# fp32r products for gather and spread of the experts, norms passed on in pairs, pooling as a band matrix

## What is computed

```
def _post_norm(h, y, g, b):
    return _layer_norm(DEEPNORM_ALPHA * h + y, g, b)

def _modulate(h, shift, scale):
    return h * (1 + scale) + shift
...
    for g, w in enumerate(POOL_SIZES):
        lo = jnp.clip(pos - w // 2, 0, n)
        hi = jnp.clip(pos + (w - w // 2), 0, n)
        mean = (cg[:, hi] - cg[:, lo]) / (hi - lo).astype(jnp.float32)[None, :, None]
        outs.append(mean - hf[:, :, g])
    y = jnp.einsum('bngc,gce->bnge', z, pool_w).reshape(b, n, d)
...
    def expert_step(acc, xs):
        y = (jax.nn.silu(t @ wg) * (t @ wu)) @ wd
        return acc + y.astype(jnp.float32) * gcol[:, None], None
...
        h = _post_norm(h, m[2] * y, ln_g[i, 0], ln_b[i, 0])
        h = _post_norm(h, m[5] * _hier_moe(_modulate(h, m[3], m[4]), *moe_p), ln_g[i, 1], ln_b[i, 1])
```

## Time and profile before

| | |
|---|---|
| median, lowest, highest of 3 runs | 2491.7, 2491.52, 2495.52 us |
| profiled execution | 2489.51 us, span 2487.7 us |
| mean granted clock of PE | 0.963 of full |
| PE / PEld / DVE / ACT busy | 93% / 64% / 40% / 18% of the span |
| DMA | 621.45 MB, mean 250 GB/s |
| first block and mixer of layer 0 | to about 1344 us |
| first experts, from the first gate product | 1400.5 to 1875.8 us |
| norm (0,1), pooling, norm (1,0), routing | 1875.8 to 1981.1 us |
| second experts | 1981.1 to 2456.3 us |
| norm (1,1) and store | 2456.3 to 2487.7 us |

### The profile page before, as it was taken

How to read it: one execution, slowest core, us unless ns; L and a number is a source line. 1 busy time by engine, 2 the same in 40 slices (tenths; PEclk the granted TensorE clock), 3 DMA queues, 4 the chain that set the end, 5 groups by cost and what they waited for, 6 DMA issues and landing times.

```text
span 2487.7 us, 31019 instructions
## 1 busy us (share of the span) xinstructions
PE 2302.5 (93%) x12984; PEld 1596.9 (64%) x12984; DVE 1003.0 (40%) x2100; ACT 457.0 (18%) x729; POOL 3.8 (0%) x12
## 2 busy tenths in 40 slices
PE   7998989998999989998997899999995699999996
PEld 6876779997876679997976544444433444444443
DVE  7888535541266335546375311111106511111112
ACT  2112114330123214334242100000000000000000
POOL 0000000000000000000000000000000000000000
PEclk9998999999999999999998899999997899999998
DMA  6435643444435724442213599999974199999991
GB/s 246 165 136 203 248 158 136 169 169 145 160 139 217 288 102 160 178 164 100 99 71 157 213 420 427 427 427 427 428 325 203 60 411 425 425 430 427 426 427 58
DMA packets 43340, 621.45 MB, mean 250 GB/s; under 512 B 4816, under 2 KB 4816, under 8 KB 5232
## 3 DMA queue, kind: packets, MB, share of 16 engines
q1 hardware_dynamic: 33984, 489.93, 48.9%
q10 hardware_dynamic: 8640, 125.83, 11.9%
q0 software_dynamic: 624, 4.39, 0.4%
HBM read 619.08 MB, written 1.05 MB: 249 GB/s over the span
## 4 chain that ended last, share of the span: by engine, by line
PE 85%; DVE 12%; issue 1%; ACT 1%; DMA 1%; DVEq 0%; SPq 0%; ACTq 0%
PE bank L525 24%; PE bank L1087 18%; PE bank L1109 9%; PE sums L1117 5%; PE bank L708 3%; PE bank L709 3%; PE bank L710 3%; PE sums L710 2%; PE sums L709 2%; PE sums L708 2%; DVE wide L1631 2%; PE bank L546 2%; DVE arena L1658 2%; PE bank L535 2%; PE bank L836 2%; PE bank L838 2%
## 5 line engine op out<-in xcount | busy, mean ns | idle before, releaser
L525 PE MATMUL bank<-h,ring 128*128 128x256 f32 x1600 | 359.6, 386 | 15.1 <-DVE h L1556 12.1
L525 PEld LDWEIGHTS bank<-h,ring 128*128 128x128 f32 x1600 | 307.0, 193 | 65.7 <-DVE h L1556 12.9
L1109 PE MATMUL bank<-ring,wide 128*64 128x512 f32 x1024 | 233.8, 598 | 0.0
L1858 DVE TENSOR_TENSOR ring_split<-ring,arena_split 128x2048 fp32r<-128x2048 f32 x64 | 143.8, 2288 | 110.6 <-ACT arena_split L1322 110.4
L2255 DVE TENSOR_TENSOR wide<-bank,wide 128x256 f32<-128x256 f32 x64 | 27.2, 425 | 394.7 <-ACT wide L1485 394.7
L2260 DVE COPY wide<-bank 128x512 f32<-128x512 f32 x64 | 44.3, 692 | 345.1 <-PE bank L1109 345.1
L1485 ACT ACTIVATE wide<-bank 128x256 f32<-128x256 f32 x64 | 24.5, 383 | 751.2 <-PE bank L1087 751.2
L708 PE MATMUL bank<-h_split,arena_split 128*128 128x256 f32 x512 | 146.6, 286 | 15.0 <-DVE ring_split L1858 15.0
L1109 PEld LDWEIGHTS bank<-ring,wide 128*64 128x64 f32 x1024 | 67.8, 136 | 130.8 <-issue 130.8
L525 PE MATMUL bank<-arena,ring 128*128 128x256 f32 x496 | 118.4, 401 | 31.3 <-DVE arena L2301 19.7
L709 PE MATMUL bank<-scratch_split,arena_split 128*128 128x256 f32 x512 | 146.2, 285 | 0.0
(11 more groups left out here) (314 smaller groups left out, 3429.4 us busy)
## 6 DMA issues: line engine op xcount, KB each, us to landing
ring<-in_stream SPq DMA_DIRECT2D x100, 2048.0 KB, 7.8
ring<-in_experts SPq DMA_DIRECT2D x98, 2048.0 KB, 10.0
arena<-in_experts SPq DMA_DIRECT2D x34, 2048.0 KB, 15.2
ring<-in_experts ACTq DMA_DIRECT2D x30, 2048.0 KB, 13.4
arena<-in_experts ACTq DMA_DIRECT2D x30, 2048.0 KB, 13.3
wide<-in_na_bias POOLq DMA_DIRECT2D x1, 1536.0 KB, 9.6
arena<-in_consts POOLq DMA_DIRECT2D x1, 1088.0 KB, 6.4
x<-in_tokens SPq DMA_DIRECT2D x1, 1024.0 KB, 6.0
```

The source lines that it names most:

```text
L525: mm = pe.matmul(dst, a, b, start=(first and i == 0), stop=(i == len(terms) - 1))
L1109: mm = pe.matmul(banks[2][64 * half:64 * half + 64, :], M["turned"][:, e % 2, at:at + 64], w[:, k, 512 * half:512 * half + 512], start=(k ...
L1858: dve.tensor_tensor(split["ring"][:, slot, 2048 * part:2048 * part + 2048], v, HI[("up", "down")[part]][:, j % 2, :].bitcast(F32), ALU.sub ...
```

## The change

- **Gather and spread in fp32r.** `wide` is now also visible as fp32r. The rows by token are kept as a high part (ACT) and a remainder `rows_low` (DVE), the gather has twice the products, all fp32r. The weight of a slot is no longer in the spread matrix: ACT sums it up beside the copy of the turned matrix, DVE makes the matrix 0/1, ACT writes `y` scaled by the weight, DVE its remainder `y_low`, and the spread takes both.
- **Norms by pairs.** Residual, sums, centring, squares (now on ACT) and scaling go by pairs of tiles (128x512), each with its own signal. Gain, shift and modulation are folded into columns by `norm_columns` once, ahead of the first residual; ACT makes `h` for tiles 0 to 5, DVE for 6 and 7, and ACT scales `x` afterwards. The router takes `h` pair by pair, and the last norm's store is four DMAs.
- **Pooling as a band matrix.** The windowed mean less the token itself is a 256x256 band matrix for each group, made on the host (1 MB, in place of 0.5 MB of counts). PE first multiplies `h` by the weights, with tokens on the output partitions, DVE copies the result (`PL["rows"]`), and PE multiplies it by the band.

```diff
+band = np.zeros((P, 4, 2, T), np.float32)
...
-    counts[:, g] = 1.0 / (hi - lo)
...
+    inside = (t[:, None] >= lo[None, :]) & (t[:, None] < hi[None, :])
+    m = np.where(inside, np.float32(1) / (hi - lo).astype(np.float32)[None, :], np.float32(0)) - np.eye(T, dtype=np.float32)
+    band[:, g] = m.reshape(2, P, T).transpose(1, 0, 2)
+return c, c2, band.reshape(P, 8 * T)
...
+    rows_low = split["smax"][:, 2:6, :]
+    slot_weight = small[:, 112:114]
+    place_split = [MS["place"], M2S["place"]]
...
+for b in range(4):
+    h_pair_ready(sp, 1, 1, b)
+    sp.dma_start(out[:, 2 * b:2 * b + 2, :], x[:, 2 * b:2 * b + 2, :]).then_inc(S.sem("stored"), 16)
+sp.wait_ge(S.sem("stored"), 4 * 16)
...
+pool.wait_ge(S.sem("h_dve"), S.value("h_dve", 0, 0))
+pool.dma_start(PL["band"], pool_band.rearrange("p (a b) -> p a b", a=8)).then_inc(S.sem("band_landed"), 16)
...
-    S.wait(pe, "added", i, s)
-    over_features(lambda j, k: x[:, k, :], [KT], "sum", "post", i, s)
-    over_features(lambda j, k: scratch[:, k, :], [KT], "sum2", "post", i, s, squares_of=("post", i, s))
+    bank = open_bank(pe, "sum", "post", i, s)
+    for b in range(4):
+        pe.wait_ge(S.sem("added"), S.value("added", i, s, b))
+        for k in (2 * b, 2 * b + 1):
+            mm = pe.matmul(bank[:, 0:T], ones, x[:, k, :], start=(k == 0), stop=(k == KT - 1))
+    filled(mm, "sum", "post", i, s)
+    bank = open_bank(pe, "sum2", "post", i, s)
+    for b in range(4):
+        pe.wait_ge(S.sem("post_squares"), S.value("post_squares", i, s, b))
+        for k in (2 * b, 2 * b + 1):
+            mm = pe.matmul(bank[:, 0:T], ones, scratch[:, k, :], start=(k == 0), stop=(k == KT - 1))
+    filled(mm, "sum2", "post", i, s)
...
+    for b in range(4):
+        h_pair_ready(pe, i, 0, b)
+        for k in (2 * b, 2 * b + 1):
+            for t in range(2):
+                mm = pe.matmul(bank[:, t * 64:t * 64 + 36], h[:, k, t * P:(t + 1) * P],
+                               prm("w_router", (i * KT + k) * 36, 36), start=(k == 0 and t == 0),
+                               stop=(k == KT - 1), skip_group_check=True)
...
+    pe.wait_ge(S.sem("rows_low"), S.value("rows_low", i, 1, 1))
...
             mm = product(bank[:, a * T:(a + 1) * T],
-                         [(M["by_token"][:, t, k * P:(k + 1) * P], placed_at[buf][:, t, :]) for t in range(2)])
+                         [(MS["by_token"][:, t, k * P:(k + 1) * P], place_split[buf][:, t, :]) for t in range(2)]
+                         + [(rows_low[:, 2 * t + k // 4, c:c + P], place_split[buf][:, t, :]) for t in range(2)])
...
-        for m in (0, 4, 1, 5, 2, 6, 3, 7):
-            a, c = 64 * (m // 4), (m % 4) * P
-            pe.matmul(sums[m // 2][:, (m % 2) * T:(m % 2 + 1) * T], M["y"][a:a + 64, c:c + P],
-                      M["turned"][a:a + 64, before, T:2 * T], start=False, stop=False, skip_group_check=True)
+        for m in range(4):
+            for part in (MS["y"], M2S["y_low"]):
+                for n in (m, m + 4):
+                    a, c = 64 * (n // 4), m * P
+                    pe.matmul(sums[n // 2][:, (n % 2) * T:(n % 2 + 1) * T], part[a:a + 64, c:c + P],
+                              MS["turned"][a:a + 64, before, T:2 * T], start=False, stop=False, skip_group_check=True)
...
-    S.wait(pe, "pooled", g)
...
+def pool_rows(g):
+    h_pair_ready(pe, 0, 1, g)
+    bank = open_bank(pe, "pool_rows", g)
+    for t in range(2):
+        mm = product(bank[:, t * T:(t + 1) * T],
+                     [(h[:, 2 * g + k, t * P:(t + 1) * P], w[:, g, k, :]) for k in range(2)])
+    filled(mm, "pool_rows", g)
+def pool_band_of(g):
+    pe.wait_ge(S.sem("pool_rows_kept"), S.value("pool_rows_kept", g))
     bank = open_bank(pe, "pool", g)
     for j in range(2):
         mm = product(bank[:, j * T:(j + 1) * T],
-                     [(w[:, g, k, j * P:(j + 1) * P], PL["z"][:, 2 * g + k, :]) for k in range(2)])
+                     [(PL["rows"][:, g, t * T + j * P:t * T + (j + 1) * P], PL["band"][:, 2 * g + t, :]) for t in range(2)])
     filled(mm, "pool", g)
+pe.wait_ge(S.sem("band_landed"), 16)
+pool_rows(0)
+pool_rows(1)
+pool_band_of(0)
+pool_rows(2)
+pool_band_of(1)
+pool_rows(3)
+pool_band_of(2)
+pool_band_of(3)
...
+            bank = take(act, "rows", i, t, half)
+            S.give(act.activation(MS["by_token"][:, t, 512 * half:512 * half + 512], bank[:, :], ACT.Copy),
+                   "rows_high", i, t, half)
...
-            act.activation(M["turned"][:, e % 2, :], banks[1][:, :], ACT.Copy)\
+            act.activation(M["turned"][:, e % 2, 0:T], banks[1][:, 0:T], ACT.Copy)\
                .then_inc(S.sem(f"moe{i}_turned"), 1)
+            act.activation(smax[:, 1, T:2 * T], banks[1][:, T:2 * T], ACT.Copy,
+                           accum_out=slot_weight[:, e % 2:e % 2 + 1]).then_inc(S.sem(f"moe{i}_weight_summed"), 1)
+            act.wait_ge(S.sem(f"moe{i}_down_done"), it * 4 + (e + 1))
+            act.wait_ge(S.sem(f"moe{i}_weight_summed"), it * 4 + (e + 1))
+            act.activation(MS["y"], banks[2][:, :], ACT.Copy, scale=slot_weight[:, e % 2:e % 2 + 1])\
+               .then_inc(S.sem(f"moe{i}_y_high"), 1)
...
+def post_norm(i, s):
+    for b in range(4):
+        act.wait_ge(S.sem("centred"), S.value("centred", i, s, b))
+        S.give(act.activation(pair_of(scratch, b), pair_of(x, b), ACT.Square), "post_squares", i, s, b)
+    root(("post", i, s))
+    last = (i, s) == (1, 1)
+    for b in range(3):
+        act.wait_ge(S.sem("scaled_by_root"), S.value("scaled_by_root", i, s, b))
+        for k in (2 * b, 2 * b + 1):
+            if last:
+                ins = act.activation(x[:, k, :], x[:, k, :], ACT.Identity, scale=prm("ln_g", 3 * KT + k),
+                                     bias=prm("ln_b", 3 * KT + k))
+            else:
+                ins = act.activation(h[:, k, :], x[:, k, :], ACT.Identity, scale=norm_col(i, s, "h_gain", k),
+                                     bias=norm_col(i, s, "h_shift", k))
+        S.give(ins, "h_act", i, s, b)
+    if last:
+        return
+    for k in range(KT):
+        if k == 6:
+            act.wait_ge(S.sem("h_dve"), S.value("h_dve", i, s))
+        ins = act.activation(x[:, k, :], x[:, k, :], ACT.Identity, scale=norm_col(i, s, "x_gain", k),
+                             bias=norm_col(i, s, "x_shift", k))
+    S.give(ins, "x_scaled", i, s)
...
-    centre(tag, x, KT, D, ("sum", *tag))
+    twice = [P, 2, T]
+    bank = take(dve, "sum", *tag)
+    mean = bank[:, 0:T].unsqueeze(1).to_broadcast(twice)
+    for b in range(4):
+        v = x[:, 2 * b:2 * b + 2, :]
+        n = S.give(dve.scalar_tensor_tensor(out=v, in0=mean, scalar=-1.0 / D, in1=v, op0=ALU.mult, op1=ALU.add),
+                   "centred", i, s, b)
+    read("centred", n, "sum", *tag)
     variance(tag, D, LN_EPS, ("sum2", *tag))
     inverse_root(tag)
-    for k in range(KT):
-        ins = dve.scalar_tensor_tensor(out=x[:, k, :], in0=x[:, k, :], scalar=prm("ln_g", (2 * i + s) * KT + k),
-                                       in1=stat[:, 1, 0:T], op0=ALU.mult, op1=ALU.mult)
+    r = stat[:, 1, 0:T].unsqueeze(1).to_broadcast(twice)
+    for b in range(4):
+        v = x[:, 2 * b:2 * b + 2, :]
+        n = S.give(dve.tensor_tensor(v, v, r, ALU.mult), "scaled_by_root", i, s, b)
+    dve.wait_ge(S.sem("scaled_by_root"), n)
+    for k in (6, 7):
+        if (i, s) == (1, 1):
+            ins = dve.tensor_scalar(x[:, k, :], x[:, k, :], prm("ln_g", 3 * KT + k), prm("ln_b", 3 * KT + k),
+                                    ALU.mult, ALU.add)
+        else:
+            ins = dve.tensor_scalar(h[:, k, :], x[:, k, :], norm_col(i, s, "h_gain", k),
+                                    norm_col(i, s, "h_shift", k), ALU.mult, ALU.add)
+    S.give(ins, "h_dve", i, s)
...
+def norm_columns():
...
+    for i, s, j in ((0, 0, 3), (0, 1, 0), (1, 0, 3)):
+        m = mod[1 if (i, s) == (0, 1) else i]
+        n = 2 * i + s
+        g, b = prm("ln_g", n * KT, KT), prm("ln_b", n * KT, KT)
+        shift, scale = m[:, 8 * j:8 * j + 8, 0], m[:, 8 * j + 8:8 * j + 16, 0]
+        dve.tensor_tensor(norm_cols[:, n, 0:KT], g, scale, ALU.mult)
+        link(dve.tensor_tensor(norm_cols[:, n, KT:2 * KT], b, scale, ALU.mult))
+        dve.tensor_tensor(norm_cols[:, n, KT:2 * KT], norm_cols[:, n, KT:2 * KT], shift, ALU.add)
+        dve.tensor_scalar(norm_cols[:, n, 2 * KT:3 * KT], g, float(ALPHA), None, ALU.mult)
+        ins = dve.tensor_scalar(norm_cols[:, n, 3 * KT:4 * KT], b, float(ALPHA), None, ALU.mult)
...
-    for k in range(KT):
-        ins = dve.tensor_scalar(x[:, k, :], x[:, k, :], prm("ln_b", (2 * i + s) * KT + k), None, ALU.add)
...
-        if b == 3:
-            n = S.give(ins, "added", i, s)
-            kind = "added"
...
+        n = S.give(ins, "added", i, s, b)
...
+norm_columns()
...
+    def keep_low(t, half):
+        dve.wait_ge(S.sem("rows_high"), S.value("rows_high", i, t, half))
+        bank = bank_of("rows", i, t, half)
```

(23 more changed lines are left out.)

99 lines of the change are left out of this document (37 added, 62 removed).

## The result

The changed kernel takes **2413.6 us** (median of 4 runs, 2408.92 to 2421.96) against 2491.6 for the kernel before (4 runs, 2491.29 to 2495.52): a ratio of 0.9687 with a 95% interval of 0.9659 to 0.9716, so 78 us or 3.1% faster. The forecast was 2412, with a range of 2392 to 2438. The profiled execution took 2408.92 us with a span of 2407.1, 80.6 less than the span before.

What follows compares the result with a forecast made beforehand. PE (14.75 us per expert) and DMA (14.73) were taken as tied in the stages, with serial ladders around them. Savings 12.3 + 13.1 + 29.5 + 13.1 + 10.2 = 78.2 us gave 2412 us, range 2392 to 2438.

Steps and rivals of the forecast that it cites:

- The stage: Each expert stage: PE catches up and runs at the DMA rate, 462.2 us instead of 475.3, 13.1 saved.
- the tail: End of each expert stage: from the last bytes landed through the closing zero products, 14.8 us.
- PE per expert: Expert stages: with fp32r gather and spread, PE needs 12.8 to 13.8 us per expert instead of 14.75.
- The cover of the turn: Expert stages: the gather of 0.96 us just covers the turn's 0.9 us wait for silu and hidden.
- Ahead of the first stage: Residual, norm, router, routing and first gathers before the first expert stage: 12.3 us saved (9 to 15).
- Between the stages: From the first stage's residual to the second stage, sums, pooling, router and gathers: 29.5 us saved (20 to 37).
- The pooling stretch: Between the stages, reciprocal to next sum: pooling by PE products takes 20.9 us instead of 31.9, 11.0 saved.
- The end: After the second stage, sums, scale and shift, and store: 10.2 us saved (8 to 13).
- Rival 1: Expert stages: DMA has room and the stage follows PE, 46 us saved per stage, total 2346; 5%.
- Rival 2: Expert stages: PE held at 14.7 us by handshake or y chain, stages give nothing, total 2438; 6%.
- Rival 3: Expert stages: fp32r products run at weight-load time, PE 15.4 to 18.4 us per expert, 2582 at 17; 4%.
- the signs named: Changed profile: expert period 14.7 us, PE waits 1 to 2, last bytes to residual 14 to 16, ladders 43 and 76.

Runs made afterwards that it cites:

- half-down runs: Changed kernel and kernel before, each loading only half of each down chunk's columns from the second turn on: 2341.0 us and 2489.7 us.
- a_unpaired: Changed kernel with the spread's products ordered one half of the array after the other instead of alternating: 2413.5 us.
- a_same: The changed kernel once more, unedited, timed beside the first experiments: 2415.4 us, ratio 0.9701 to the kernel before.
- a_norms_only: Changed kernel with fp32 gather, spread and y and DVE pooling as before, only the norms by pairs left: 2444.2 us.
- a_same2: The changed kernel once more, unedited, timed beside the last three experiments: 2415.2 us, ratio 0.9699 to the kernel before.

## Why the prediction was right, point by point

**The stage: right in kind, 2.8 us short.** The period is set by the DMA rate, PE gains 1.55 us per expert and waits for its chunks, and the lag behind the data shrinks: all as said, and the two half-down runs show both ceilings. The length came out at 465.0 instead of 462.2. The DMA view of the changed kernel from 1826 to 1838 us in 40 slices, rate (as the earlier trace rows):

```profile
GB/s 328 492 382 437 382 492 382 492 382 492 382 492 328 492 382 492 273 382 273 218 273 164 273 55 218 55 55 0 55 0 0 0 0 0 0 0 0 0 0 0
```

The last slice with any traffic ends at 1834.7 us, 449.6 after the first gate product (forecast 447.4): 2.2 of the 2.8 us missed. The rest is the tail, 15.4 us instead of 14.8, by the chain:

```profile
1830.46 6.89 PE bank L1125 x32
...
1840.07 3.61 PE bank L1147 x16
...
1845.22 1.22 PE sums L1157 x16
1846.44 3.65 PE sums L1187 x8
1850.11 0.89 DVE x L2240 x2
```

The last gate product starts with no wait behind the expert before it, and gate and up end 2.7 us behind the last byte, where the working let them end at +2: PE still lags a little at the very end. The working has two slips of its own. Its tail, added up again, is 15.25 us and not 14.8 (2 + 1.6 + 1.5 + 3.6 + 1.4 + 1.5 + 3.65); the steps behind gate and up took 12.8 us where it lists 13.25, the two spreads being shorter than 1.5 each. And the earlier trace rows show traffic up to 1852.0 us, not 1850.3, so by the same reading the lag before was 23.8 us and not 25.5. The forecast that PE would have caught up "after some ten experts" was too slow: PE first waits for a chunk at 1477.7 us, after seven.

**PE per expert: inside its bounds.** 1.15 us for the gather (0.96 booked) and for the spread (0.96 to 1.92). The spread's 0.07 us a product, against 0.11 in the order of `a_unpaired`, says that its pairs do run side by side. The cover of the turn held: PE waits for it only in the last 4 of the 32 experts, which have no gather to cover it, 3.8 us in all.

**Ahead of the first stage: 15.6 instead of 12.3.** The second sum is the step that was mis-sized. The working gave it 6.55 us, half clock, on the ground of the earlier trace rows; it took 3.71, and the step as a whole gave 5.0 where 2.3 were said. PE now pauses 1.6 us ahead of it instead of 3.7. That the shorter pause kept the clock up is likely and not shown: in the kernel before, the second sum at 1936.83 comes behind a pause of the same 3.7 us and takes 3.71 us at a granted clock of 1.00. Gathers gave 3.9 (3.3 said), the routing lost 0.6 (1.3 said): the four subtractions stand in the chain with 0.69 and 1.89 us, and most of that was made up around them. Scale, shift and router gave 7.0, as said. The 1.0 booked for the first sum came too, but outside the 15.6: the sum starts without a pause (0.96 us before), only PE reached it 1.2 us later than in the kernel before, hence the -0.2 in the table.

**Between the stages: 33.1 instead of 29.5**, and again the clock: the two sums of the first norm gave 4.0 and 5.0 (3.4 and 3.0 said), since both run at 3.7 us. The first gathers gave 4.6 (3.3 said), the router 6.3 (7.0 said). The pooling stretch took 20.1 us (20.9 said), the third band product did wait for its bank and the last copy of rows (chain: 0.53 of issue, 0.65 small copies, 0.89 residual), but the six products at half clock that the working took for granted show only in some executions (12.08 + 3.69 us here, 13.05 + 5.28 in `a_same`). One attribution was wrong though its size was right: the 11.0 us stood under pooling, as the band matrix's, and `a_norms_only` shows that half of it comes from the folded columns of the norm ahead. On top of the other parts, the band matrix is worth 3 to 5 us.

**The end: 11.4 instead of 10.2**, again with two errors that partly cancel: the two sums gave 8.9 (6.4 said), by the same clock, scaling and shift gave 1.7 (2.1 said), and the store 0.8 (1.7 said): it ends 3.6 us behind the last scaled tile, where 2.6 were said.

**The rivals.** Rival 1, room in the DMA queues, would have been 2346; the run in which bytes were taken away gave 2341, so it was priced well and its condition did not hold. Rival 2, the lag not taken back, 2438: the run with fp32 gather and spread stands at 2435.7, which is that case. Rival 3, products at the time of their weight loads: the gather's 8 products take 1.15 us, 0.14 each, with loads of 0.19 in the earlier trace rows; loads run beside products here too. The Trainium skill (TensorE: Matmul & The Clock Gate, "Part 3"), which lets a load overlap only a product of another row group, is contradicted by this also for the gather; the measurement decides. Of the signs named, the period and the waits, the end of the data to the residual (15.4; 14 to 16 said) came as said, the first sum to the first gate product (40.0; 43 said) and the residual to the second stage (72.1; 76 said) came lower, the second not in every execution: 75.9 in `a_same`, 76.7 in `a_same2`.

That last point qualifies the hit. The profiled execution was the fastest of the four. `a_same2`, at 2414.0 us nearer to their median, has 4.6 us more between the stages, and two other kernels 6 us more in the first block. The median of 2413.6 is closer to the forecast than the parts were to theirs.

## What to carry to other kernels

Where an engine and the DMA rate are tied, making the engine faster pays only with the lag it had piled up; work it out from when the last byte lands, and test both ceilings by taking bytes away, before and after. The larger gain of this change (46 of 77 us) lay in the serial ladders around the stages, where each step passed on by pairs shortens the path by itself, and where the sums on PE, which now come after shorter pauses, all ran at the full clock in the changed kernel. Before a seemingly idle product is deleted, look at what runs next on PE: here, filling a pause ahead of the last step shortened the span by 7.2 us and removing the work behind it by 5.6, one profile each.
